# A hybrid RWKV-7/GLA encoder step: the stationary operand of the inverse's powers, from two 64x64 tiles to one 128x128 with four diagonal blocks

## What is computed

```python
def step(S, inp):
    r_t, k_t, v_t, w_t, kk_t, a_t = inp
    sa = jnp.einsum('bhij,bhj->bhi', S, -kk_t)
    S = S * w_t[:, :, None, :] + sa[..., None] * (kk_t * a_t)[:, :, None, :] + v_t[..., None] * k_t[:, :, None, :]
    return S, jnp.einsum('bhij,bhj->bhi', S, r_t)
```

## Time and profile before

| | us |
|---|---|
| median of three runs | 1382.58 |
| the profiled execution, its time | 1385.92 |
| its span | 1384.1 |
| before the recurrence, 0 to 540.5 | 540.5 |
| recurrence, 540.5 to 698 (its last steps reach 708) | 157.5 |
| merge of the branches, output projection, router, 698 to 850 | 152.0 |
| experts and the rest, from 850 | 534.1 |

### The profile page before, as it was taken

How to read it: one execution, slowest core, us unless ns; L and a number is a source line. 1 busy time by engine, 2 the same in 40 slices (tenths; PEclk the granted TensorE clock), 3 DMA queues, 4 the chain that set the end, 5 groups by cost and what they waited for, 6 DMA issues and landing times.

```text
span 1384.1 us, 28164 instructions
## 1 busy us (share of the span) xinstructions
PE 1330.7 (96%) x12133; PEld 983.3 (71%) x12133; DVE 700.7 (51%) x1131; ACT 492.9 (36%) x797; POOL 164.3 (12%) x217
## 2 busy tenths in 40 slices
PE   5999999999999998999999999999999999998997
PEld 1788999999999997988888998844444444433443
DVE  2423234563235665565676576625455444544454
ACT  2424235545666565565654342201000100000113
POOL 2000000000012233443313001000000000000000
PEclk9999999999999999899999999999999999999999
DMA  9556533224442220000152666899999999999993
GB/s 344 183 193 220 182 82 88 77 77 139 136 130 79 62 77 25 5 4 4 54 156 86 207 187 224 320 408 408 404 428 426 427 426 427 428 426 426 427 427 150
DMA packets 132921, 310.63 MB, mean 224 GB/s; under 512 B 13314, under 2 KB 98536, under 8 KB 119864
## 3 DMA queue, kind: packets, MB, share of 16 engines
q1 hardware_dynamic: 122078, 285.86, 54.9%
q10 hardware_dynamic: 7546, 15.58, 3.1%
q0 software_dynamic: 3168, 7.33, 1.5%
HBM read 299.88 MB, written 12.79 MB: 226 GB/s over the span
## 4 chain that ended last, share of the span: by engine, by line
PE 50%; DMA 7%; DVE 1%; issue 1%; ACT 1%; SPq 0%; DVEq 0%; ACTq 0%
PE bank L3063 13%; PE bank L2880 7%; PE bank L3087 6%; DMA lower<-in_expert_w_up 4%; PE bank L3107 4%; PE bank L2910 3%; DMA upper7b<-in_expert_w_up 2%; PE bank L1800 2%; PE bank L502 2%; PE bank L3074 1%; PE bank L3037 1%; PE bank L1856 1%; PE bank L1864 1%; PE bank L2918 1%; PE bank L1798 1%
## 5 line engine op out<-in xcount | busy, mean ns | idle before, releaser
L963 PE MATMUL bank<-upper2end 128*128 128x272 f32 x3168 | 413.6, 290 | 0.2 <-DVE upper2end L1169 0.2
L963 PEld LDWEIGHTS bank<-upper2end 128*128 128x128 f32 x3168 | 400.6, 189 | 17.6 <-issue 16.5
L3063 PE MATMUL bank<-upper7b 128*64 128x512 f32 x784 | 230.7, 596 | 6.3 <-issue 3.8
L1169 DVE TENSOR_TENSOR upper2end<-upper,upper2end 128x1024 fp32r<-128x1024 f32 x66 | 84.7, 1284 | 249.4 <-ACT upper2end L722 249.2
L3063 PEld LDWEIGHTS bank<-upper7b 128*64 128x64 f32 x784 | 69.8, 137 | 115.5 <-issue 115.3
L3063 PE MATMUL bank<-lower,upper7b 128*64 128x512 f32 x240 | 108.5, 596 | 3.9 <-issue 2.4
L2748 ACT ACTIVATE lower<-bank 128x256 f32<-128x256 f32 x32 | 12.3, 384 | 274.4 <-PE bank L3074 274.4
L3087 PE MATMUL bank<-upper7b,lower 128*64 128x512 f32 x352 | 106.3, 595 | 0.9 <-DVE lower L3510 0.9
L3575 DVE TENSOR_TENSOR lower<-lower,bank 128x1024 f32<-128x1024 f32 (+1 forms) x70 | 82.8, 1215 | 46.0 <-PE bank L3107 43.4
L2880 PE MATMUL bank<-upper_r 128*128 128x272 f32 (+2 forms) x768 | 101.8, 291 | 0.0
L2880 PEld LDWEIGHTS bank<-upper_r 128*128 128x128 f32 x768 | 97.6, 188 | 2.9 <-issue 1.5
(11 more groups left out here) (451 smaller groups left out, 1877.5 us busy)
## 6 DMA issues: line engine op xcount, KB each, us to landing
upper7b<-in_expert_w_gate SPq DMA_DIRECT2D x20, 2048.0 KB, 23.1
upper7b<-in_expert_w_up SPq DMA_DIRECT2D x19, 2048.0 KB, 28.4
upper7b<-in_expert_w_down SPq DMA_DIRECT2D x19, 2048.0 KB, 24.2
upper<-in_w_in SPq DMA_DIRECT2D x66, 512.0 KB, 3.8
lower<-in_w_ada SPq DMA_DIRECT2D x23, 1024.0 KB, 6.6
lower<-in_expert_w_down SPq DMA_DIRECT2D x7, 2048.0 KB, 24.9
lower<-in_expert_w_gate SPq DMA_DIRECT2D x6, 2048.0 KB, 21.9
lower<-in_expert_w_up SPq DMA_DIRECT2D x6, 2048.0 KB, 28.5
```

What stands on the lines that cost most here:

```text
L963: m = mm(psum[s][:, c, 0:HALF], w_part[s][:, k, :], h_part[:, k, c * HALF:(c + 1) * HALF], start=k == 0 and w_part is w_high and h_part is ...
L1169: ve.tensor_tensor(w_rest[u % 2], w_slot[u % 2], w_high[u % 2].bitcast(F32), ALU.subtract).then_inc(w_split, 1)
L3063: m = nc.tensor.matmul(GU_BANK[s][64 * b:64 * b + 64, :], x_t[:, k, s * BLK:(s + 1) * BLK], w[:, k, :], start=k == 0, stop=k == KD - 1)
```

## The change

The stationary operand `pw` becomes 128 columns wide per pair: `pw[:, j]` is a 128x128 matrix with four blocks of 32 on its diagonal. The blocks outside a head's own 64 columns are zeroed once by two memsets on VectorE. Each power is then spread by three ScalarE operations on 64 partitions each (both blocks of the first head, the first of the second head) and one VectorE operation on 64 partitions (`last_block`, the last block of the second head). For the prompt chunks `power` on TensorE then issues 8 matmuls with the full 128x128 operand instead of 16 with 64x64; the moving operands and the results are the same in size. The sample chunk keeps its tiles of 32x32. The counts of the waits on `pw_out` follow, and the tile `u0` moves to another region of SBUF to make room.

```diff
-        pw = S4.take(8, CH)
+        pw = S4.take(8, P)
...
-        u0 = S4.take(8, CH)
...
+        u0 = S6.take(8, CH)
...
             if c:
-                v.wait_ge(pw_out, 10 * c)
+                v.wait_ge(pw_out, 20 * c + 2)
...
-                for b in range(2):
-                    nc.scalar.activation(pw[:, :, 32 * b:32 * b + 32], pt_turned, ACT.Copy, scale=own_half[:, b:b + 1]
+                for h, b in ((0, 0), (0, 1), (1, 0)):
+                    p, at = HEADS[h], CH * h + 32 * b
+                    nc.scalar.activation(pw[p, :, at:at + 32], pt_turned[p], ACT.Copy, scale=own_half[p, b:b + 1]
                                          ).then_inc(pw_out, 1)
...
+            def last_block(c, k):
+                p = HEADS[1]
+                v.wait_ge(p_out, 5 * c + k + 1)
+                if c and not k:
+                    v.wait_ge(inv_mm, inv_count(c - 1, "5"))
+                nc.vector.tensor_scalar(pw[p, :, 96:P], pt_turned[p], own_half[p, 1:2], None, ALU.mult
+                                        ).then_inc(pw_out, 1)
+
             def power(c, k):
...
                 nc.vector.transpose(pt_turned.rearrange("p j n -> p (j n)"), out[:, :, 0:32]).then_inc(p_out, 1)
+                last_block(c, k)
...
+            for h, p in enumerate(HEADS):
+                nc.vector.memset(pw[p, :, CH * (1 - h):CH * (2 - h)], 0.0).then_inc(pw_out, 1)
+            last_block(0, 0)
             power(0, 1)
...
             inverse(0)
+            last_block(1, 0)
...
                     inverse(c + 1)
                     if c + 1 < NCH:
+                        last_block(c + 2, 0)
...
-                pe.wait_ge(pw_out, 10 * c + 2 * k)
+                pe.wait_ge(pw_out, 20 * c + 4 * k + 2)
...
                 for j in range(8):
-                    for r in QUADS[0:4:2] if c == NCH else HEADS:
-                        lhs = pw[r, j, 0:tokens(c)]
+                    for h, r in enumerate(QUADS[0:4:2] if c == NCH else (slice(0, P),)):
+                        lhs = pw[r, j, CH * h:CH * h + 32] if c == NCH else pw[:, j]
```

## The result

The changed kernel took 1450.26 us, the median of four runs (1447.25 to 1453.38), against 1384.26 for the kernel before: a ratio of 1.047 (95% interval 1.044 to 1.050). That is 66 us slower; 38 were forecast, with a range that ended at 1436. Repeated later in six more runs the same kernel took 1436.49 (1430.58 to 1444.8) against 1383.91: 1.039 (1.036 to 1.042). So the direction holds, and part of the size is not fixed. Which chip the first four runs had is not on record, so a part of the difference between the two series may be the chip's. The ten runs of the changed kernel lie between 1431 and 1453 us; of the 48 runs of the kernel before that stood beside them and the other experiments, the lowest was 1380.5 and the highest 1392.9.

What follows compares the result with a forecast made beforehand. TensorE's instruction stream was taken to bound chunks 1 to 7, the relay chunk 0. Chunks 1 to 7 30.5, chunk 0 5.8, chunk 1's cold power 1.0, chunk 8 0.7: 38.0 us on 1382.6, forecast 1421 us, range 1411 to 1436.

Steps and rivals of the forecast that it cites:

- What bounds the kernel: In the recurrence, TensorE's own instruction stream sets the pace in chunks 1 to 7; in chunk 0 the engine-to-engine handover does.
- the shift one for one: A later end of the recurrence moves the kernel's end by the same amount, with no DMA transfer hiding it.
- The price of a power, +0.78: On TensorE, 16 loads of 128 columns at 107 ns take 1.71 us instead of 0.93, five powers per chunk.
- the change of tiling: On TensorE, 0.15 us per change; two boundaries per chunk, formerly free, now pay it: +0.30 us per chunk.
- The relay: TensorE over VectorE and ScalarE back to TensorE: third ACTIVATE adds 0.41 to 0.42 us, mostly covered; 0.15 us wait per chunk.
- no TensorE step waits closely for what stands behind `last_block`: On VectorE, `last_block` delays what is queued behind it by 0.3 us, which no TensorE step waits for closely.
- its 2.7 for the clock: The half-clock terms in chunk 0 and chunk 1, counted as 2.7 us that might not come.
- Cold power 2, +1.7: In chunk 0, power 2 at half clock takes 3.6 us in the new form: +1.7 us if it stays cold.
- cold power 1 of chunk 1, +1.0: Power 1 of chunk 1 at half clock takes 3.6 us instead of 1.85, 1.0 us more than already counted.
- the first rival: The clock falls further: chunks 1 to 7 get 0.79, 40 us more, 1461 us; chance 0.08.

Runs made afterwards that it cites:

- the wide matmuls alone: Changed kernel with only two ScalarE spread operations and no `last_block`, odd heads' powers left zero, TensorE still multiplying 128x128: 1427.94 us, ratio 1.032 to the kernel before.
- the spread's 11.3: Changed kernel with its whole new spread, but TensorE multiplying with 64x64 operands again: 1399.15 us, ratio 1.013 to the kernel before.
- the added 512 columns: Changed kernel plus unread identity multiplications of 512 moving columns: in chunk 0 1433.12 us, ahead of chunk 1's first powers 1433.48, in both places 1434.74.
- the half-column kernel: Kernel before, with powers 2 to 4 of the prompt chunks moving only 32 columns: 1385.00 us against 1383.91, ratio 1.002.
- a near copy: Changed kernel with VectorE's `last_block` moved behind the copy and the sum of the inverse: four runs of 1434.7, 1440.4, 1461.1 and 1512.1 us.

## Why the prediction was wrong

**What bounds the kernel, and the shift one for one: right.** The steps behind the recurrence come 61 to 62 us later, from first to last.

**The price of a power, +0.78: right in kind, a little small for the step.** 16 loads of 128 columns take 1.93 us start to start with the change of tiling, where 1.71 + 0.15 = 1.86 was forecast. The share of the loads in the total follows from the wide matmuls alone. Two executions of one kernel give the price of half clock: the changed kernel's spans are 1445.4 and 1430.9 us at 78.5 and 44.4 us of half clock, 14.5 / 34.1 = 0.43 us for each, the same as the line through all ten executions. The wide matmuls alone have a span 43.4 us over that of before at 30.7 us more half clock: 43.4 - 13.2 = 30.2 us, or 0.76 for each of 40 powers. The forecast for the same parts was 5 x 0.78 + 0.30, over 7 chunks, 29.4, and some 2.6 in chunk 0: 32.

**The relay: mis-sized, and two waits left out.** In my sum it had some 4 us; alone it costs 17 by the medians and 11 at the same half clock. The step that failed here is the sentence that no TensorE step waits closely for what stands behind `last_block`: `diagonal_blocks` and the next power do, 0.4 us each time. `last_block` was also priced at 346 ns. 32 of the 45 took 353, but 13 took 0.52 to 1.29 us, and each of these began while a GpSimd operation ran and ended shortly after it (two that began in the last 0.2 us of one stayed at 353):

```profile
614.29 1.27 POOL L1532 TENSOR_TENSOR upper<-lower,upper 64x512 f32<-64x512 f32 x1
614.42 1.28 DVE L1675 TENSOR_SCALAR upper<-upper,lower 64x256 f32<-64x256 f32 x1
```

GpSimd ends at 615.56, the block at 615.70. In the changed kernel a part of the relay is hidden, as the longer powers cover it: with the wide matmuls' 30.2 and the spread's 11.3 (12.8 of span less 3.4 x 0.43) the parts sum to 41.5, while the whole, without its half clock, is 61.3 - 58 x 0.43 = 36.4 us. My sum without its 2.7 for the clock was 35.3. So the terms at full clock came out right as a total, but in part by luck: the loads were put some 2 us too high (32 against 30.2) and the relay some 2 too low (about 4 against the 6.2 that are left of the 36.4).

The Trainium skill bears on that pair of rows: "SBUF — State Buffer", section "Who interferes with whom", describes a port pair that VectorE and GpSimd share by an exclusive lock, with the loser blocked for the whole instruction. It counts a tensor-scalar among the operations that can take the pair. The rows above fit it, the operation ending 0.15 us after GpSimd's. I had read it and did not apply it to the operation that the change adds.

**The clock: the term that failed.** "Cold power 2, +1.7, cold power 1 of chunk 1, +1.0" supposed that the half clock lasts as long as before, 20.5 us. It lasted 78.5 us in the first profiled execution and 44.4 in the second: 25 and 10 us of time more than those 20.5. With the 36.4 us at full clock the first makes up the 61.3 by which the span grew; the second gives 46.8 - 10.3 = 36.5, the same rest, as it must, since the price comes from these two; the other eight executions bear it out by lying on the same line. This is the mechanism of the first rival, at another place than I put it: not chunks 2 to 7 at 0.79, but chunks 0 and 1 at 0.5 from end to end. I gave it 0.08 and let the range end below it.

**Why the clock stays down.** What the traces show: the first fall is no doing of the wide powers. It comes in all 17 profiled executions, between 537.8 and 542.9 us, while TensorE stands idle ahead of power 1 or within 1 us after that. What differs is when it ends. In the kernels with narrow powers of full length each stretch of half clock in the recurrence ended after 3.4 to 14 us. With wide powers there are stretches of 31, 48 and 72 us with TensorE busy nearly throughout. In the stretches with wide powers there are 23 returns. Before each of them TensorE had run, up to the return or to 1.2 us before it, a piece without a wide power: `keys_by_queries` with `solved`, `new_state` or `y_inside`, or `off_left` and `right_side`, or the added 512 columns. But such a piece is not enough: the one from 567.8 to 574.6 us, 6.8 us long, brought the clock back in the second execution of the changed kernel (568.5 us on) and left it at half in the first. At half clock a wide power takes 3.6 us and comes after every shorter such piece, of about 3.7 us. That wide powers hinder the return is shown by these kernels; by what property of theirs is not: the half-column kernel shows that narrow powers with fewer moving columns also lower the mean clock, and no run varies this in a wide power. That the scatter of the times is the scatter of the half clock is shown by the ten executions; what decides in a single one whether a piece brings the return stays open. So does why the first stretch begins at 539 in one and at 541 or 542 us in others, and when a fall comes in chunks 2 to 7.

## What to carry to other kernels

Merging two operands that use two tiles of the array at once into one block-diagonal operand halves the matmuls, and where the weight load is the longer part, as with 64 moving columns, it nearly doubles the time of the step: price it by the columns of a load on one tile, 1.93 against 1.08 us here. Before lengthening loads over short streams, look at how TensorE gets its clock back around them, and take as the range's far end the whole stretch at half clock. For an operation put into another engine's queue, follow who waits for each instruction behind it, also in other loops, and who holds the memory port when it starts.

## What the runs showed of the hardware that I had not expected

- With powers of 128x128 loads and 32 or 64 moving columns in it, work that kept TensorE busy nearly throughout ran at half clock for 72 us in one execution and for 31 in another of the same program.
- The time of one program with such a stream scatters between executions, 1431 to 1453 us for the changed kernel and 1435 to 1512 for a near copy, by 0.43 us for each us of half clock.
- A VectorE tensor-scalar of 64x256 from SBUF to SBUF took 0.35 us, or 0.52 to 1.29 us when it started during a GpSimd operation; in 12 of these 13 cases it ended 0.15 to 0.16 us after it.
- Loads of 128 rows and 64 columns on two column tiles cost the same as 64 rows: 1.06 us for 32 of them.
